# A four-layer hybrid trunk on one core: feed-forward up projections with the activations stationary, 512 weight columns moving, and the gated result turned by TensorE

## The reference, cut to what matters

```
def swiglu_ffn(h, w1, w3, w2):
    return (jax.nn.silu(h @ w1) * (h @ w3)) @ w2

x = x + (1 + gt1) * y
h = rms_norm(x, norm2_w[i]) * (1 + sc2) + sh2
x = x + (1 + gt2) * swiglu_ffn(h, ffn_w1[i], ffn_w3[i], ffn_w2[i])
```

## Time and profile before

| | us |
|---|---|
| median of 3 runs | 1759.0 (1755.16 to 1759.3) |
| span of the profiled execution | 1761.2 |
| its own time | 1761.2 |
| TensorE matmuls busy | 1697.8 (96%) |
| VectorE busy | 1294.6 (74%) |
| ScalarE busy | 886.5 (50%) |
| HBM read | 343.91 MB, 196 GB/s over the span |

### The profile page before, as it was taken

The page is one execution under the profiler, slowest core; times in us unless marked ns, Lnnn a source line. Parts: engine busy times, 40 slices in busy tenths (PEclk is TensorE's granted clock), DMA queues, the critical chain, the costliest instruction groups (busy, mean ns, idle before and its releaser), DMA issues.

```text
span 1761.2 us, 36364 instructions
## 1 busy us (share of the span) xinstructions
PE 1697.8 (96%) x15387; PEld 1592.4 (90%) x15387; DVE 1294.6 (74%) x1898; ACT 886.5 (50%) x1253; POOL 21.3 (1%) x62
## 2 busy tenths in 40 slices
PE   7999999999999978899999998999999999999998
PEld 6998789999987866599999996999999998999998
DVE  6897887899764564579996566799958977767553
ACT  3765764444423233354444656444436768644442
POOL 4000000000000000000000000000000000000000
PEclk8999999999999999999999998999999999999999
DMA  9564456999823400239997340599964632548551
GB/s 334 162 189 136 132 209 241 316 339 348 312 63 120 135 27 3 73 104 363 354 342 273 117 162 11 181 350 357 350 224 132 188 112 92 171 147 280 179 196 62
DMA packets 217795, 347.32 MB, mean 197 GB/s; under 512 B 8416, under 2 KB 175024, under 8 KB 217632
## 3 DMA queue, kind: packets, MB, share of 16 engines
q1 hardware_dynamic: 215856, 344.22, 57.7%
q10 hardware_dynamic: 1648, 0.43, 0.1%
q0 software_dynamic: 128, 0.33, 0.1%
HBM read 343.91 MB, written 1.05 MB: 196 GB/s over the span
## 4 chain that ended last, share of the span: by engine, by line
PE 84%; DVE 7%; DMA 3%; ACT 3%; issue 2%; ACTq 0%; DVEq 0%
PE psum_dve L443 28%; PE psum_act L443 28%; PE psum_acc L443 27%; DMA ring<-in_ffn_w_dram 2%; DVE w_lo L1321 1%; PE psum_act L446 1%; DVE arena L1596 1%; PE psum_dve L446 1%; DMA arena<-in_ada_b_dram 1%; DVE arena L1690 1%; ACT w_hi L1844 1%; DVE arena L1292 1%; DVE arena L1460 0%; DVE arena L1498 0%; ACTq L2194 0%
## 5 line engine op out<-in xcount | busy, mean ns | idle before, releaser
L1844 ACT ACTIVATE w_hi<-ring 128x1024 fp32r<-128x1024 f32 x432 | 458.7, 1062 | 376.9 <-DMA ring<-in_ffn_w_dram 238.9
L1321 DVE TENSOR_TENSOR w_lo<-ring,w_hi 128x1024 fp32r<-128x1024 f32 x432 | 517.0, 1222 | 172.9 <-ACT w_hi L1844 169.4
L443 PE MATMUL psum_dve<-h_lo,w_hi 128*128 128x256 f32 x1216 | 332.7, 280 | 0.0
L443 PE MATMUL psum_act<-h_lo,w_hi 128*128 128x256 f32 x960 | 258.3, 281 | 0.0
L1292 DVE SCALAR_TENSOR_TENSOR arena<-ring,vcol,arena 128x512 f32<-128x512 f32 x336 | 239.1, 748 | 4.5 <-DMA ring<-in_ada_w_dram 0.8
L443 PEld LDWEIGHTS psum_dve<-h_lo,w_hi 128*128 128x128 f32 x1216 | 225.8, 188 | 0.2
L443 PE MATMUL psum_acc<-g_hi,w_hi 128*128 128x256 f32 x704 | 201.0, 286 | 0.0
L443 PE MATMUL psum_acc<-g_hi,w_lo 128*128 128x256 f32 x704 | 197.6, 281 | 0.0
L443 PE MATMUL psum_acc<-g_lo,w_hi 128*128 128x256 f32 x704 | 197.6, 281 | 0.0
L443 PE MATMUL psum_dve<-h_hi_ffn,w_hi 128*128 128x256 f32 x704 | 196.4, 281 | 0.8 <-DVE w_lo L1321 0.8
L443 PE MATMUL psum_dve<-h_hi_ffn,w_lo 128*128 128x256 f32 x704 | 196.3, 281 | 0.0
(11 more groups left out here) (312 smaller groups left out, 3325.7 us busy)
## 6 DMA issues: line engine op xcount, KB each, us to landing
ring<-in_ffn_w_dram SPq DMA_DIRECT2D x132, 1024.0 KB, 7.2
ring<-in_ada_w_dram SPq DMA_DIRECT2D x96, 1024.0 KB, 7.2
ring<-in_m_in_w_dram SPq DMA_DIRECT2D x48, 1024.0 KB, 5.4
ring<-in_m_out_w_dram SPq DMA_DIRECT2D x16, 1024.0 KB, 5.0
ring<-in_r_w_rkv_dram SPq DMA_DIRECT2D x12, 1024.0 KB, 5.5
ring<-in_f_qkvf_w_dram SPq DMA_DIRECT2D x12, 1024.0 KB, 5.3
ring<-in_r_out_w_dram SPq DMA_DIRECT2D x4, 1024.0 KB, 5.1
ring<-in_f_out_w_dram SPq DMA_DIRECT2D x4, 1024.0 KB, 4.9
```

The source lines that it names most:

```text
L443: return nc.tensor.matmul(o, l, r, start=start, stop=stop, skip_group_check=True)
L1321: tell(V.tensor_tensor(o, raw, hi, ALU.subtract), split_ready, hold=False)
L1844: tell(A(o, raw, ACT.Copy), hi_ready)
```

## The change: what it does

The operands of the up projections change places. A 128-token half of the activations is stationary, and 512 columns of weights move, so a result has tokens on partitions and hidden columns in a row. A load now holds 512 columns of `w1` and the same 512 of `w3` for 256 rows, in two DMAs of 2 KB pieces; a unit is one row tile k with both. Hidden columns are taken in 6 groups (`UP`): five of 512, with 8 units each, and one of 256, whose 4 loads of before's size become 2 loads, 4 units, of 1 KB pieces. A group fills four banks (two token halves, `w1` and `w3`); even groups use `psum_acc`, odd ones `psum_act` and `psum_dve`. A unit is 12 matmuls of 512 columns. In the first group the high parts go ahead of the low parts.

After a group ScalarE applies Silu and VectorE multiplies (`gated`), into `gx`, by token. TensorE turns this in 128 x 128 transposes (`turn_gated`) into a bank, after row tile 3 of the next group, and ScalarE and VectorE split it from the bank (`high`, `low`). The last group is turned before row tile 1 of the down projection.

```
+            for n in range(KF):
+                j, i = divmod(n, 4)
+                load_up(l, j, i)
+                if pending and n > 1 and n % 8 != 7:
+                    load_ada(*pending.pop(0))
...
+            def up_unit(l, j, k, w, c):
+
+                for tt in range(TT):
+                    h = h_parts(k, slice(tt * P, (tt + 1) * P))
+                    banks = up_banks(j)[2 * tt:2 * tt + 2]
+                    for n, (lh, part) in enumerate(((h[0], w[0]), (h[0], w[1]), (h[1], w[0]))):
+                        for b, moving in zip(banks, up_moving(part, j, c)):
+                            last = mm(b[:, :], lh, moving, k == 0 and n == 0, k == KD - 1 and n == 2)
+                    if k == KD - 1 and tt == 0:
+                        last.then_inc(up_full, 1)
+                return last
...
+            def turn_gated(l, j):
+
+                for q in range(min(2, KF // 2 - 2 * j)):
+                    pe.wait_ge(up_gated, 2 * UP * l + 2 * j + 2)
+                    b = up_banks(j)[q + (2 if j == UP - 1 else 0)]
+                    for f in (2 * q, 2 * q + 1):
+                        for tt in range(TT):
+                            last = tr(b[:, (f % 2 * TT + tt) * P:(f % 2 * TT + tt + 1) * P], gx[:, (2 * j + tt) % 4, f * P:(f + 1) * P])
+                    last.then_inc(g_turned, 1)
...
             def ffn(l):
                 note(("ffn", l))
-                for i in range(KF // 2):
-                    if i == 0:
-                        first_tiles("act", more="dve")
-                    else:
-                        two_tiles("act")
-                        two_tiles("dve")
+                pe.wait_ge(acc_free, 4 * count["down"])
+                for j in range(UP):
+                    if j == 1:
+                        all_read_out()
+                    if j >= 2:
+                        pe.wait_ge(g_split, KF // 2 * l + 2 * j - 2)
...
+                        if j and k == 3:
+                            turn_gated(l, j - 1)
                 reduced = dict(ffn_reduced(l))
+                pe.wait_ge(g_split, KF // 2 * l + 2 * (UP - 1))
 
                 def ready(k):
+                    if k == 1:
+                        turn_gated(l, UP - 1)
+                    if k == 4:
+                        pe.wait_ge(g_split, KF // 2 * (l + 1))
...
+                for j in range(UP):
+                    stream(group_end(f0, j) - 1 + UNITS)
+                    gated(j)
+                    stream(group_end(f0, j) + (3 if j < UP - 2 else 1) + UNITS)
+                    for i in range(2 * j, min(2 * j + 2, KF // 2)):
+                        low(i)
```

More of the change, by code:

```diff
@@ L36 @@
 E_HALF = math.exp(-0.5)
+UP = -(-KF // 4)
 UNIT = 1024
@@ L290, in load_down, with load_up @@
             how((*key, i), (slice(0, SLOT), w[256 * i:256 * i + 256, :].rearrange("(k p) n -> p k n", p=P), P, D))
+        def load_up(l, j, i):
+            width = min(NB, DFF - NB * j)
+            deep = UNIT // width
+            split(("up", l, j, i), *((slice(m * UNIT, (m + 1) * UNIT), rows(t[w][l][deep * P * i:deep * P * (i + 1), :], NB * j, width), P, width)
+                                     for m, w in enumerate(("ffn_w1", "ffn_w3"))))
         def ffn_parts(l):
@@ L348, in unit_view @@
         def unit_view(n, u):
+            if len(loads[n]) == 2:
+                return slot(n).rearrange("p (m c) -> p m c", m=2)[:, :, u * NB:(u + 1) * NB]
             if loads[n][0][3] == 256:
@@ L356, in trunk, with group_end, turned_bank @@
         assert all(ada_place[l, 4 * m + 3] == ada_place[l, 4 * m] + 3 for l in range(DEPTH) for m in range(6))
+        def group_end(f0, j):
+            return f0 + min(KD * (j + 1), 2 * KF)
+        def turned_bank(i):
+            j, q = divmod(i, 2)
+            banks = psum_acc if j % 2 == 0 else [*psum_act, *psum_dve]
+            return banks[q + (2 if j == UP - 1 else 0)]
         def part_sum(l, m):
@@ L694, in x_out, with up_banks, up_moving, up_high @@
                 close_bank(who, last)
+            def up_banks(j):
+                return psum_acc if j % 2 == 0 else [*psum_act, *psum_dve]
+            def up_moving(w, j, c):
+                if j < KF // 4:
+                    return [w[:, m * NB:(m + 1) * NB] for m in range(2)]
+                return [w.rearrange("p (m c n) -> p m c n", m=2, c=2)[:, :, c, :]]
+            def up_high(j, k, w, c):
+                for tt in range(TT):
+                    h = h_high(k)[:, tt * P:(tt + 1) * P]
+                    banks = up_banks(j)[2 * tt:2 * tt + 2]
+                    for part in w:
+                        for b, moving in zip(banks, up_moving(part, j, c)):
+                            mm(b[:, :], h, moving, k == 0 and part is w[0], False)
@@ L1426, in low, with gated @@
                     tell(V.tensor_tensor(flat(g_lo[:, v, :]), gx[:, i % 3, :], flat(g_hi[:, v, :]).bitcast(F32), ALU.subtract), g_split, hold=False)
[L1427 to L1435, removed]
+                def gated(j):
+                    for tt in range(TT):
+                        n = 2 * j + tt
+                        banks = psum_acc if j % 2 == 0 else [*psum_act, *psum_dve]
+                        b = banks[2 * tt + 1][:, :] if j < KF // 4 else banks[2 * tt][:, 256:512]
+                        v = gx[:, n % 4, 0:b.shape[1]]
+                        dve.wait_ge(up_silu, 2 * UP * l + n + 1)
+                        tell(V.tensor_tensor(v, v, b, ALU.mult), up_gated)
+                def low(i):
+                    v = slice(2 * i, 2 * i + 2)
+                    b = turned_bank(i)
+                    dve.wait_ge(g_hi_ready, KF // 2 * l + i + 1)
+                    tell(V.tensor_tensor(flat(g_lo[:, v, :]), b[:, :], flat(g_hi[:, v, :]).bitcast(F32), ALU.subtract), g_split, hold=False)
+                for j in range(UP):
[4 more added lines that the diff above has]
+                        low(i)
                 if l in (1, 2):
@@ L1879, in ffn, with silu @@
                 f0 = first_unit("up", l, 0, 0)
-                def high(i):
[L1882 to L1894, removed]
+                def silu(j):
+                    for tt in range(TT):
+                        n = 2 * j + tt
+                        banks = psum_acc if j % 2 == 0 else [*psum_act, *psum_dve]
+                        b = banks[2 * tt][:, :] if j < KF // 4 else banks[2 * tt][:, 0:256]
+                        act.wait_ge(up_full, 2 * UP * l + n + 1)
+                        if n >= 4:
+                            act.wait_ge(g_turned, KF // 2 * l + 2 * (j - 1))
+                        tell(A(gx[:, n % 4, 0:b.shape[1]], b, ACT.Silu), up_silu)
+                def high(i):
+                    act.wait_ge(g_turned, KF // 2 * l + i + 1)
+                    tell(A(flat(g_hi[:, 2 * i:2 * i + 2, :]), turned_bank(i)[:, :], ACT.Copy), g_hi_ready)
+                for j in range(UP):
+                    stream(group_end(f0, j) - 1 + UNITS)
+                    silu(j)
+                    if j == UP - 1:
+                        log_exp_table()
+                    stream(group_end(f0, j) + (3 if j < UP - 2 else 1) + UNITS)
+                    for i in range(2 * j, min(2 * j + 2, KF // 2)):
+                        high(i)
                 for k, part in ffn_reduced(l):
```

43 lines of the change are left out of this document (34 added, 9 removed).

## The result

| | before | after |
|---|---|---|
| median, us | 1758.55 (4 runs, 1755.16 to 1759.3) | 1769.28 (4 runs, 1767.28 to 1773.77) |
| span of the profiled execution | 1761.2 | 1772.0 |
| ratio | | 1.0063, 95% 1.0045 to 1.0082 |

A forecast was written before the change was run, and what follows sets the result against it. TensorE was taken to bound layer 3, with VectorE and DMA within 10 us of it in layers 0 to 2. Gains 5.2 + 8.6 less 3.5 for the clock gave 10.3 us off 1761.2: 1751, median 1749, range 1741 to 1764.

The forecast's parts named there:

- the term 217 ns: Up projections on TensorE: 528 matmuls of 512 columns a layer at 217 ns each, 114.6 us a layer.
- Rival (d): Up matmuls: 512 columns cost as much a column as 256, 237 ns a matmul; 21 us slower, 1780; chance 0.07.
- Transposes: Turning the gated result on TensorE: 44 a layer at 0.115 us, plus 0.6 for changes of kind, 5.6 us a layer.
- Rival (e): Transposes don't overlap among fp32r matmuls, 298 ns each, 13.1 us for 44; total 1770; chance 0.04.
- Sum for layer 3: Layer 3's up stretch, bound by TensorE alone: 114.6 + 5.6 = 120.2 us against 125.4, a gain of 5.2 us.
- VectorE: Up stretch: its work stays, one idle time of 3.49 us goes, continuous work ends unit 47 at 121.4 us from the start.
- DMA: Up weight loads: resume some 3.4 us sooner, and 2 KB pieces save 0.25 us a load, bounds 0 and 0.32.
- the new wait: Before row tile 1 of the down projection, TensorE waits 2 to 3 us for VectorE's last product in layers 0 to 2.
- the clock: Behind that TensorE idle time the granted clock falls in one or two of layers 0 to 2, costing 3.5 us.
- Rival (c): Loads no faster; layer 0's last turn 129.8 us after up stretch start s; 1 us slower, 1755 to 1765; chance 0.27.
- Rival (f): Inside up stretches TensorE waits for `g_lo` before groups 2 to 5, 12 to 18 us; 1752 to 1768; chance 0.10.

The follow-up runs named there:

- m_quiet: Trunk left out, only series of matmuls of several types and widths with nothing beside them; fp32r 226.7 ns at 512 columns, 120 at 256, 111 at 128.
- m_series: Trunk left out, 16 series of 48 fp32r matmuls, varying width and operand reuse; 226.7, 173.5, 146.5 and 120.0 ns at 512, 384, 320 and 256 columns.
- a_short: Changed kernel with 30 low matmuls of 512 columns a layer left out of the up projections; 1747.34 us in one run (before 1754.59).
- a_256: Changed kernel with each 512-column up matmul made as two of 256 columns, all else kept; 1781.69 us, ratio 1.0152.

## Why the prediction was wrong

**The step that failed** is the reading "the 11 ns as the price of a weight load that doesn't fit under 107 ns. Under 213 ns of columns it fits", and with it the term 217 ns, 114.6 us a layer. Measured are 233.6 ns, 123.3 us, 8.7 us a layer more. Of the 16.6 ns by which the term was off, about 10 are the cost beside the columns that I took to vanish and that stays at every width (226.7 alone, shown by m_quiet and m_series) and 7 are the kernel's own addition at 512 columns, whose cause is open. The evidence was taken from the wrong type: the float32 rows of 215 ns a pass are right for float32 (214.5 in m_quiet), but carry no word on fp32r. The same rows with the difference carried over, 215 + 11, would have given 226 ns, 124.9 us of TensorE a layer, within 0.5 us of before.

**Rival (d) came out** in direction, with half its size (11 us slower, where it had 21): 233.6 lies above its 227 and under its 237, and it had 0.07. Its mechanism, a cost that goes with columns, is not what m_series shows. The loss goes with matmuls in the series, and in the kernel two of 256 columns have 24 ns beside their columns where one of 512 has 20, so doubling the width gave back 4 of the 20 ns that I counted on.

**Transposes: right.** 5.6 us a layer forecast, 4.4 in the stretch and 0.4 to 0.5 in the down projection measured, 0.109 to 0.113 each. Rival (e) is out; its 1770 is nearly the measured time, by luck. The Trainium skill (TensorE: Matmul & The Clock Gate, Part 4) gives some 275 ns for one in a kernel, beside a figure for bf16 and without naming float32. As the length of one record the runs agree, 0.27 us; as the price of one more they don't, 0.109 in a group of eight and 116 ns (342.6 - 226.7) between two fp32r matmuls. The prediction multiplied it by 44 as a price, though it then went by the trace's row.

**Sum for layer 3:** 123.3 + 4.4 = 127.7 against 125.4, 2.3 us more, where 5.2 less was forecast; layers 1 and 2 went the same way. Layer 0 grew by 0.9 only, because its stretch before was the longest (126.76 us, of which TensorE was busy 126.00).

**VectorE, DMA, the new wait, the clock.** Loads with 2 KB pieces are faster, 0.12 to 0.17 us a load in layer 3 against 0.25 taken, within the bounds. Rival (c) is out: it had layer 0's turn at s + 129.8, and in a_short it stands at s + 125.0. The Trainium skill's line rate from 512 B on (DMA: Bandwidth & Descriptors, opening table) doesn't agree with 323 GB/s over the stretch with 1 KB pieces and 340 over that with 2 KB. The wait behind unit 47's split is real at the forecast's pace (a_short), 1.0 to 2.5 us long and at the forecast time to 1.1 us, and the clock fell in one of three layers. In the changed kernel it is not there, since TensorE arrives 7.5 us later (s + 130.5 instead of 123.0). Rival (f) did not happen: TensorE waits for nothing inside the stretches. a_short came out 7.2 us under before in one run (before itself ranges from 1751.41 to 1759.27), where the forecast was 10.3. So the rest of the working held as far as one run tells, and the one term of TensorE's pace turned 10 us of gain into 11 of loss.

## What to carry to other kernels

Where an engine is bound by the number of its instructions, ask whether the cost beside the columns is one of fit or one of each instruction, and take it from rows of the same type: a float32 row says nothing of fp32r. A saving that is the difference of two near prices (237 and 217 here) needs the point from which it turns worked out and its chance set by how well that one price is known, not by how many other terms are. When operands change places and the result has to be turned back, the turning (here 5 us a layer) is certain and the saving (2 us) is not.

## What the runs showed of the hardware

- fp32r matmuls, each with its weight load of 128 columns, cost by themselves their columns at 2.4 GHz and 13.2 to 13.5 ns at 256, 320, 384 and 512 columns, 19.6 at 448, with a floor of 111 ns at 192 and 128; bf16 took 215.7, 109 and 56 ns at 512, 256 and 128.
- In the kernels the same instructions run at other paces: 117.4 and 118.7 ns at 256 columns in two layers of before, 120.0 in a_256, and 233.6 at 512 against 226.7 alone. A difference of 3% in the pace of one instruction form between a series and a kernel was worth 3.6 us a layer here.
- Narrower stationary tiles are not faster at 512 moving columns: 64 and 96 columns took 230 ns (L71 above), 32 took 232, 128 took 226.7. At 256 moving columns they are: 64 and 32 took 113 to 114 ns, 128 took 120.
- Neighbours busy in SBUF, with 408 GB/s of DMA, moved no fp32r or bf16 series by 1 ns.
- In a_short idle times of 0.9 and 1.2 us left the granted clock at 1.00, and one of 2.4 us was followed by a fall, as those of 2.31 and 2.52 us were before. The length alone doesn't decide: in before an idle time of 2.28 us (at 1088.0) left it at 1.00, and in the changed kernel ones of 1.32 and 0.94 us (at 718.4 and 720.3), among matmuls of 64 x 64, stood around a fall to 0.50 that lasted 3.4 us.
